# Eight projection strips that start from raw tokens instead of normalized ones

## The chip, the cores and the metric

The kernel runs as one program on one core of one Trainium2 chip. The metric is the time of one execution in microseconds (us), as the device measures it. Three executions of the kernel before gave a median of 1279.75 us (1279.38 to 1280.37). The engines are TensorE (PE in the profile, its weight loads PEld), VectorE (DVE), ScalarE (ACT), GpSimd (POOL) and SyncE (SP), which issues most of the DMA transfers.

## The reference, cut to what matters

Two transformer blocks run on 512 tokens of width 1024. Only the beginning of the first one bears on this change:

```python
def rmsnorm(x, gain):
    y = x * lax.rsqrt(jnp.mean(x * x, axis=-1, keepdims=True) + NORM_EPS)
    return y * gain

h = rmsnorm(x, mix_norm[l])          # x: 512 tokens x 1024
proj = h @ w_in[l]                   # 1024 x 3840
q, k, v, su, sv, g_a, g_b = jnp.split(proj, splits, axis=-1)
# chunked_spatial_gating(su, sv, ...):
u = jax.nn.gelu(su)
v = rmsnorm(jax.nn.gelu(sv), sgu_gain)
```

Everything is fp32 and is computed to more than one rounded pass of the matmul: each operand is split into a rounded part ("high") and a rest ("low"), and three products are added, high x high, low x high and high x low.

## The kernel before, in words

Activations lie transposed: 128 features on the partitions, 512 tokens along a row, 8 such tiles `k` for the width of 1024. A weight strip `n` is 1024 x 128 numbers. Its way is: SP loads it into `w_raw` (two slots, two transfers of 256 KB), DVE rounds it into `w_high` (`make_high`, L365), POOL subtracts to get `w_low` (`make_low`, L370), and PE runs 8 x 3 matmuls of 512 columns (`product`, L391 to L393). `w_high` and `w_low` have four slots. SP may load strip `n` once `w_low` of strip `n - 2` is made. The semaphores `high_made`, `low_made` and `strip_used` count these steps. Every engine works through a list that is written out in the program, and waits at semaphores; nothing reorders it.

The start runs so. Tokens come in four pieces `x_tok` of 128. DVE and ACT sum their squares, ACT makes the four columns of roots `x_root`, DVE and ACT multiply the tokens by them, and PE turns the result (`row_turn`, L864). ACT multiplies by the gain `mix_gain` while it rounds to `h_high` (L1658), DVE makes `h_low` (L2197). Besides, PE turns the raw tokens too (`raw_turn`, L853), since the residual `x_t` is wanted later. Then PE runs strips 0 to 7 (the `su` and `sv` columns), with some small transposes between them: the rows of constants and the 16 meta tokens before strip 1 (L898 to L903), the sum of the meta tokens' squares before strip 2 (L910), the mixing weights after strip 5 (L922). ACT applies GELU straight from PSUM to `uv` (L1671). For strips 4 to 7 (`sv`) a second norm follows: ACT squares (L1679), POOL adds two of them at a time (L664, with `make_low` of strip 10 between the two additions), and PE sums over partitions (`sv_sums`, L939 and L941) after the first three `k` of strip 9. Strips 8 to 13 are `k`, `v` and `q`. Four banks of PSUM, `ps[:, n % 4, :]`, are used in turn by strips 0 to 7, so that strip 4 has to wait until bank 0 has been read.

## Time and profile before

| what | value |
|---|---|
| median of three executions | 1279.75 us |
| the profiled execution | 1279.36 us |
| its span, first to last instruction | 1277.6 us |
| PE busy | 1257.2 us (98%) |
| DVE, ACT, POOL busy | 710.7, 467.3, 627.4 us |
| mean granted TensorE clock | 0.999 |

The profiled execution lies 0.39 us under the median, and 1.76 us of it lie outside the span. PE is busy from its first real work to the end, so the time is what PE has to do, plus the stretches in which it stands still. The beginning, about 30 us, and the stretch from 65 to 73 us are where it stands still near this change.

### The profile page before, as it was taken

The page shows a single profiled execution, that of the slowest core. Times are in us where ns is not written, and L with a number is a line of the kernel's source. Part 1 is how long each engine was busy: PE and PEld are TensorE (multiplying, and loading weights), DVE is VectorE, ACT ScalarE, POOL GpSimd, SP SyncE. Part 2 cuts the span into 40 slices and gives each one's busy share as a digit, 9 for nine tenths or more (in the row PEclk, how much of TensorE's full clock was granted, in tenths as well). Part 3 has the DMA queues.
Part 4 walks back from the last instruction along what each step waited for, and adds up shares of the span by engine and source line. Part 5 has one row for each costly group of instructions (what it writes and reads, how often), then busy time and mean ns, then how long its engine had stood idle before and what let it go on. Part 6 is the DMA issues. An engine that isn't in the chain of part 4 may idle for free.

```text
span 1277.6 us, 19955 instructions
## 1 busy us (share of the span) xinstructions
PE 1257.2 (98%) x6772; PEld 1032.4 (81%) x6772; DVE 710.7 (56%) x1380; ACT 467.3 (37%) x1010; POOL 627.4 (49%) x418
## 2 busy tenths in 40 slices
PE   7999999999999999999999999999999999999998
PEld 6877777877788888888888888888888888888876
DVE  5236654566855455443224788778643665665641
ACT  4233433412422222221113566566402555555531
POOL 5442333338354434445663153444347877777722
PEclk9999999999999999999999999999999999999999
DMA  7322222223232333233333221111133322222213
GB/s 205 100 66 70 81 81 78 57 88 109 83 115 82 99 99 97 84 90 97 102 91 100 67 56 44 49 33 50 50 98 95 96 79 79 78 78 78 66 34 99
DMA packets 190611, 105.42 MB, mean 83 GB/s; under 512 B 19174, under 2 KB 186444, under 8 KB 190556
## 3 DMA queue, kind: packets, MB, share of 16 engines
q1 hardware_dynamic: 189748, 102.82, 28.4%
q0 software_dynamic: 432, 0.69, 0.2%
q10 hardware_dynamic: 376, 1.18, 0.2%
q8 instruction: 33, 0.54, 0.2%
q14 instruction: 22, 0.18, 0.1%
HBM read 102.57 MB, written 2.10 MB: 82 GB/s over the span
## 4 chain that ended last, share of the span: by engine, by line
PE 90%; DVE 5%; ACT 2%; issue 1%; POOL 1%; DMA 1%; ACTq 0%; DVEq 0%
PE ps L391 20%; PE ps L392 20%; PE ps L393 20%; PE ps L422 9%; PE ps L1453 1%; PE ps L1535 1%; PE ps L1537 1%; PE ps L1536 1%; PE ps L1484 1%; PE ps L1464 1%; PE ps L1208 1%; PE ps L404 1%; PE ps L405 1%; PE ps L408 1%; DMA x_tok<-in_x_dram 1%
## 5 line engine op out<-in xcount | busy, mean ns | idle before, releaser
L370 POOL TENSOR_TENSOR w_low<-w_raw,w_high 128x1024 fp32r<-128x1024 f32 x180 | 440.1, 2448 | 445.5 <-DVE w_high L365 440.3
L391 PE MATMUL ps<-h_high,w_high 128*128 128x512 f32 x810 | 326.4, 403 | 0.5 <-DVE h_low L524 0.4
L392 PE MATMUL ps<-h_low,w_high 128*128 128x512 f32 x810 | 319.9, 395 | 0.0
L393 PE MATMUL ps<-h_high,w_low 128*128 128x512 f32 x810 | 318.8, 394 | 0.0
L365 DVE CAST w_high<-w_raw 128x1024 fp32r<-128x1024 f32 x183 | 152.4, 834 | 111.8 <-DMA w_raw<-in_w_down_dram 34.1
L391 PEld LDWEIGHTS ps<-h_high,w_high 128*128 128x128 f32 x810 | 152.2, 188 | 37.7 <-issue 3.0
L393 PEld LDWEIGHTS ps<-h_high,w_low 128*128 128x128 f32 x810 | 152.3, 188 | 34.8
L392 PEld LDWEIGHTS ps<-h_low,w_high 128*128 128x128 f32 x810 | 152.1, 188 | 33.1 <-issue 1.7
L1788 ACT ACTIVATE z<-ps,cv 128x512 f32<-128x512 f32 x42 | 32.7, 778 | 148.3 <-PE ps L393 148.3
L2407 DVE SCALAR_TENSOR_TENSOR z<-ps,cv,z 128x511 f32<-128x511 f32 x42 | 31.5, 749 | 92.8 <-ACT z L1788 92.8
L392 PE MATMUL ps<-m_low,w_high 128*128 128x512 f32 x176 | 69.4, 395 | 0.0
L393 PE MATMUL ps<-m_high,w_low 128*128 128x512 f32 x176 | 69.4, 395 | 0.0
L391 PE MATMUL ps<-m_high,w_high 128*128 128x512 f32 x176 | 69.4, 394 | 0.0
L422 PE MATMUL ps<-h_high,w_high 128*128 128x264 f32 x304 | 64.8, 294 | 0.3 <-ACT nv_end L2096 0.3
L422 PE MATMUL ps<-h_high,w_low 128*128 128x264 f32 x304 | 61.7, 284 | 0.0
L422 PE MATMUL ps<-h_low,w_high 128*128 128x264 f32 x304 | 61.5, 284 | 0.0
L770 POOL TENSOR_TENSOR nb<-rel,mask 128x128 f32<-128x128 f32 (+1 forms) x96 | 53.4, 599 | 0.2 <-DMA rel<-in_rel_bias_dram 0.2
L422 PEld LDWEIGHTS ps<-h_high,w_high 128*128 128x128 f32 x304 | 48.4, 189 | 5.2 <-issue 2.5
L2041 ACT ACTIVATE np_<-ps 128x256 f32<-128x256 f32 (+1 forms) x32 | 15.7, 491 | 93.2 <-PE ps L1468 93.2
L422 PEld LDWEIGHTS ps<-h_low,w_high 128*128 128x128 f32 x304 | 47.0, 188 | 0.0
L422 PEld LDWEIGHTS ps<-h_high,w_low 128*128 128x128 f32 x304 | 46.9, 188 | 0.0
L2714 DVE TENSOR_SCALAR ne<-ne,nm 128x272 f32<-128x272 f32 (+2 forms) x64 | 46.2, 762 | 1.1
(393 smaller groups left out, 2392.4 us busy)
## 6 DMA issues: line engine op xcount, KB each, us to landing
...
```

The source lines that it names most:

```text
L365: dve.tensor_copy(w_high[:, n % RING, :], w_raw[:, n % RAW, :]).then_inc(high_made, 1)
L370: pool.tensor_tensor(w_low[:, n % RING, :], w_raw[:, n % RAW, :], w_high[:, n % RING, :].bitcast(F32), ALU.subtract).then_inc(low_made, 1)
L391: pe.matmul(acc, wh, mh, start=first and k == 0, stop=False)
L392: pe.matmul(acc, wh, ml, start=False, stop=False)
L393: done = pe.matmul(acc, wl, mh, start=False, stop=last and k == tiles - 1)
L404: pe.matmul(ps[:, banks[o], :], w_high[:, slot, at], mh, start=k == 0, stop=False)
L422: done = pe.matmul(ps[:, bank + h, 0:HALF], wt, mt[:, k, h * HALF:h * HALF + HALF], start=one_, stop=end)
L770: pool.tensor_tensor(to, half_tiles(rel[:, h, :], r, n), half_tiles(mask[:], m, n), ALU.add)\
L1788: act.activation(z[:, m, :], src, ACT.Identity, scale=cv[:, bass.ds(i * 2 + (C_CONV + 2 * 2 * FT + ct), 1)], bias=cv[:, bass.ds(i * 2 + (C ...
L2041: act.activation(np_[:, a:a + n, :, t % 2 * P:(t % 2 + 1) * P], turned(n), ACT.Copy)\
L2407: dve.scalar_tensor_tensor(z[:, m, 1:S], src[:, 0:S - 1], cv[:, bass.ds(i * 2 + (C_CONV + 2 * FT + ct), 1)], z[:, m, 1:S], ALU.mult, ALU.a ...
L2714: p = dve.tensor_scalar(ne[:, t % 2, h, 0:w], ne[:, t % 2, h, 0:w], nm[:, t % 2, 2, h:h + 1], None, ALU.mult)
```

## The change

The tokens' roots are a factor of each column of the result, since `(x * root) @ w` is `(x @ w) * root`. The changed kernel therefore multiplies the raw tokens, times the gain, and puts the roots to the finished columns. In detail:

- PE turns the raw tokens once, in two halves of 256 tokens (`turn_half`). The turned tokens lie in banks 4 to 7. ACT rounds them times the gain into `a_high` (buffers that are otherwise unused until later), DVE makes `a_low`, ACT copies `x_t`.
- Strips 0 and 1 run as matmuls of 256 columns (`raw_pass`): both strips on the first half, then the second half is turned, then both strips on the second half. Strips 2 to 7 run at 512 columns on `a_high` and `a_low`.
- Token pieces 2 and 3 are loaded behind strips 0 and 1 on SP's queue, strip 2 ahead of the small rows of constants.
- In the middle of strip 2 stand the transposes of constants and meta tokens, and four fp32 matmuls that spread the four columns `x_root` over 128 partitions as rows. DVE copies these to `v_f`.
- For each of the strips 0 to 7 DVE multiplies the PSUM bank by `v_f` into `uv` (semaphore `sv_normed`), and ACT applies GELU to `uv` in place. PE's waits for a free bank are now on `sv_normed`.
- Behind the multiplications of strips 0 to 3, two at a time, DVE and ACT make the eight tiles of the normalized tokens `h_high` and `h_low` (`norm_dve`, `norm_highs`), which strips 8 and following use.
- `make_high` of strips 5 to 11 stands ahead of the multiplications of strips 1 to 7 on DVE; strip 11's was behind the loop before.

The diff, with removed code left out where it is only replaced (it is shown above):

```diff
--- before.py
+++ after.py
+HALF_S = S // 2
+RAW_PARTS = 2 * KT
...
-            for k in range(KT):
-                act.wait_ge(s["norm_scaled"], 8 * t - 4 + k + 1)
+            norm_highs(act, t, n, high)
+        def norm_highs(act, t, n, high, ks=(0, KT)):
+            for k in range(*ks):
+                act.wait_ge(s["norm_scaled"], 8 * t + k + 1)
                 act.activation(high(k), scaled[:, k % 2, 0:n], ACT.Copy).then_inc(s["norm_high"], 1)
...
+        def norm_dve(dve, t, src, gain, by, n, high, low, ks=(0, KT)):
+            for k in range(ks[0], ks[1] + 1):
+                if k < ks[1]:
+                    if 8 * t + k >= 2:
                         dve.wait_ge(s["norm_low"], 8 * t + k - 1)
-                    dve.scalar_tensor_tensor(scaled[:, k % 2, 0:n], src(k), col(gain + k), root[:, 0, 0:n],
+                    dve.scalar_tensor_tensor(scaled[:, k % 2, 0:n], src(k), gain(k), by[:, 0:n],
                                              ALU.mult, ALU.mult).then_inc(s["norm_scaled"], 1)
-                if k >= 1:
+                if k > ks[0]:
                     dve.wait_ge(s["norm_high"], 8 * t + k)
                     dve.tensor_tensor(low(k - 1), scaled[:, (k - 1) % 2, 0:n], high(k - 1).bitcast(F32),
...
+        def of_half(h, k):
+            return ps[:, 4 + k // 2, k % 2 * HALF_S:(k % 2 + 1) * HALF_S]
+        def raw_at(parts, h, k):
+            return parts[:, k, h * HALF_S:(h + 1) * HALF_S]
...
-            sp.dma_start(x_tok[:, 2, :], x[0, 2 * P:3 * P, :]).then_inc(s["x_rest_in"], 16)
             sp.wait_ge(s["x_in"], 32)
             for n in range(RAW):
                 load_strip(sp, n)
+            for t in (2, 3):
+                sp.dma_start(x_tok[:, t, :], x[0, t * P:(t + 1) * P, :]).then_inc(s["x_rest_in"], 16)
+            load_strip(sp, RAW)
...
-            for n in range(RAW, 4):
-                load_strip(sp, n)
-            sp.wait_ge(s["in_turned"], KT + 3)
+            load_strip(sp, RAW + 1)
+            sp.wait_ge(s["norm_sq"], 4)
             sp.dma_start(ws_raw[:], w_s[0].rearrange("g i j -> i g j")).then_inc(s["meta_in"], 16)
...
+            def turn_half(h):
+                pe.wait_ge(s[("x_in", "x_rest_in")[h]], 32)
+                if h == 0:
+                    pe.wait_ge(s["cols_ready"], 1)
+                for b in range(4):
+                    if h:
+                        pe.wait_ge(s["x_ready"], b + 1)
+                    for k in (2 * b, 2 * b + 1):
+                        for t in range(2):
+                            mm = pe.transpose(ps[:, 4 + b, (k % 2 * 2 + t) * P:(k % 2 * 2 + t + 1) * P],
+                                              x_tok[:, 2 * h + t, k * P:(k + 1) * P], ident[:])
                     mm.then_inc(s["in_turned"], 1)
-            pe.wait_ge(s["norm_scaled"], 2)
+            def raw_pass(h, n, k, w, part, first=False, last=False):
+                return pe.matmul(ps[:, n, h * HALF_S:(h + 1) * HALF_S], w[:, n, k * P:(k + 1) * P], raw_at(part, h, k),
+                                 start=first, stop=last)
+            turn_half(0)
+            pe.wait_ge(high_made, 1)
+            for k in range(KT):
+                pe.wait_ge(s["raw_high"], k + 1)
+                raw_pass(0, 0, k, w_high, a_high, first=k == 0)
             for k in range(4):
...
+                pe.wait_ge(s["raw_low"], k + 1)
+                raw_pass(0, 0, k, w_high, a_low)
+            pe.wait_ge(low_made, 1)
             for k in range(KT):
-                t = pe.transpose(ps[:, 6, k * META:(k + 1) * META], meta_tok[:, k * P:(k + 1) * P],
-                                 ident[0:META, 0:META])
-            t.then_inc(s["in_turned"], 1)
+                raw_pass(0, 0, k, w_low, a_high)
+            pe.wait_ge(high_made, 2)
+            for k in range(KT):
+                raw_pass(0, 1, k, w_high, a_high, first=k == 0)
+            for k in range(4, KT):
+                pe.wait_ge(s["raw_low"], k + 1)
+                raw_pass(0, 0, k, w_high, a_low, last=k == KT - 1)
+            for k in range(KT):
+                raw_pass(0, 1, k, w_high, a_low)
             pe.wait_ge(low_made, 2)
...
+            for k in range(KT):
+                raw_pass(0, 1, k, w_low, a_high, last=k == KT - 1)
+            turn_half(1)
+            for k in range(KT):
+                pe.wait_ge(s["raw_high"], KT + k + 1)
+                for n in range(2):
+                    raw_pass(1, n, k, w_high, a_high, first=k == 0)
+                    raw_pass(1, n, k, w_low, a_high)
+                pe.wait_ge(s["raw_low"], KT + k + 1)
+                for n in range(2):
+                    mm = raw_pass(1, n, k, w_high, a_low, last=k == KT - 1)
+                    if k == KT - 1:
+                        mm.then_inc(strip_used, 1)
+            def raw(k):
+                return a_high[:, k, :], a_low[:, k, :]
+            for n in range(2, N_QKV):
                 pe.wait_ge(low_made, n + 1)
+                if n >= 4:
+                    pe.wait_ge(s["sv_normed"], n - 3)
+                cut = 4 if n == 2 else KT
+                mm = product(pe, ps[:, n % 4, :], n, 0, P, KT, raw, ks=(0, cut))
                 if n == 2:
-                    pe.wait_ge(s["meta_ready"], 1)
-                if n >= 4:
-                    pe.wait_ge(s["gelu_done"], n - 3)
-                product(pe, ps[:, n % 4, :], n, 0, P, KT, hx).then_inc(strip_used, 1)
+                    pe.wait_ge(s["x_ready"], 8)
+                    pe.wait_ge(s["consts_in"], 16 * N_CONST)
+                    pe.wait_ge(s["more_in"], 16 * N_EARLY)
...
+                    pe.wait_ge(s["norm_root"], 4)
+                    for t in range(4):
+                        mm = pe.matmul(ps[:, 5, t * P:(t + 1) * P], x_root[:, t:t + 1].broadcast_to([P, P]), ident[:],
+                                       start=True, stop=True)
+                    mm.then_inc(s["in_turned"], 1)
+                    mm = product(pe, ps[:, n % 4, :], n, 0, P, KT, raw, ks=(cut, KT))
+                mm.then_inc(strip_used, 1)
+                if n == 2:
+                    pe.wait_ge(s["norm_sq"], 12)
+                    pe.matmul(ps[:, 4, 0:META], ones[:], sq[:, 1, 0:META], start=True, stop=True)\
+                        .then_inc(s["norm_sum"], 8)
                 if n == 5:
...
+            pe.wait_ge(s["norm_low"], 16)
             pe.wait_ge(s["more_in"], 16 * N_MORE)
...
                 if m == 1:
-                    pe.wait_ge(s["gelu_done"], 8)
+                    pe.wait_ge(s["sv_normed"], 8)
...
-            act.dma_start(x_tok[:, 3, :], x[0, 3 * P:S, :]).then_inc(s["x_rest_in"], 16)
             act.preload_act_table_set("natural_log_exp_and_others")
             act.wait_ge(s["ones_set"], 2)
...
+            def raw_highs(h):
+                for k in range(KT):
+                    act.wait_ge(s["in_turned"], 1 + 4 * h + k // 2 + 1)
+                    act.activation(raw_at(a_high, h, k), of_half(h, k), ACT.Copy, scale=mix_gain[:, k:k + 1])\
+                        .then_inc(s["raw_high"], 1)
+            def keep_x(h):
+                for b in range(4):
+                    act.wait_ge(s["raw_low"], KT * h + 2 * b + 2)
+                    act.activation(x_t[:, 2 * b:2 * b + 2, h * HALF_S:(h + 1) * HALF_S],
+                                   ps[:, 4 + b, :].rearrange("p (k q) -> p k q", q=HALF_S), ACT.Copy)\
+                        .then_inc(s["x_ready"], 1)
+            def square_token(t):
                 act.activation(xh_tok[:, t, :], x_tok[:, t, :], ACT.Square, accum_out=x_sum[:, t:t + 1])\
                     .then_inc(s["norm_sq"], 1)
...
+            act.wait_ge(s["cols_ready"], 1)
+            raw_highs(0)
+            keep_x(0)
+            act.wait_ge(s["x_in"], 32)
+            square_token(0)
+            raw_highs(1)
+            act.wait_ge(s["x_rest_in"], 32)
+            square_token(2)
+            keep_x(1)
+            act.wait_ge(s["norm_sq"], 4)
+            act.activation(x_root[:], x_sum[:], ACT.Ln, bias=eps[:, 0:1], scale=1.0 / D).then_inc(s["norm_root"], 2)
+            act.wait_ge(s["norm_root"], 2)
+            act.activation(x_root[:], x_root[:], ACT.Exp, scale=-0.5).then_inc(s["norm_root"], 2)
+            act.wait_ge(s["in_turned"], 11)
...
+            norm_highs(act, 0, META, lambda k: h_high[:, k, 0:META])
             for n in range(8):
-                act.wait_ge(strip_used, N_SGU + n + 1)
-                act.activation(uv[:, n, :], ps[:, n % 4, :], ACT.Gelu_apprx_tanh).then_inc(s["gelu_done"], 1)
+                act.wait_ge(s["sv_normed"], n + 1)
+                act.activation(uv[:, n, :], uv[:, n, :], ACT.Gelu_apprx_tanh).then_inc(s["gelu_done"], 1)
+                if n < 4:
+                    norm_highs(act, 1, S, hh, (2 * n, 2 * n + 2))
...
+            def raw_lows(h, ks):
+                for k in ks:
+                    dve.wait_ge(s["raw_high"], KT * h + 2 * (k // 2) + 2)
+                    dve.scalar_tensor_tensor(raw_at(a_low, h, k), of_half(h, k), mix_gain[:, k:k + 1],
+                                             raw_at(a_high, h, k).bitcast(F32), ALU.mult, ALU.subtract)\
+                        .then_inc(s["raw_low"], 1)
             def square_token(t, ready):
                 dve.wait_ge(ready, 32)
                 dve.tensor_tensor_reduce(xh_tok[:, t, :], x_tok[:, t, :], x_tok[:, t, :], 1.0, 0.0, ALU.mult, ALU.add,
                                          x_sum[:, t:t + 1]).then_inc(s["norm_sq"], 1)
+            make_high(dve, 0)
+            raw_lows(0, range(4))
+            make_high(dve, 1)
+            raw_lows(0, range(4, KT))
             square_token(1, s["x_in"])
-            scaled_tokens(0, (0, 1))
+            make_high(dve, 2)
+            raw_lows(1, range(KT))
             square_token(3, s["x_rest_in"])
...
+            make_high(dve, 3)
+            dve.wait_ge(s["in_turned"], 10)
             dve.tensor_copy(cv[:], ps[:, 7, 0:C_V + V_ROWS]).then_inc(s["cols_ready"], 1)
             dve.wait_ge(s["cols_ready"], 2)
             dve.tensor_scalar(aq_gain[:], col(V_AQ), HD ** -0.5, None, ALU.mult).then_inc(s["gain_ready"], 1)
             dve.tensor_scalar(nq_gain[:], col(V_NQ), HD ** -0.5, None, ALU.mult).then_inc(s["gain_ready"], 1)
-            make_high(dve, 3)
             for k, v in enumerate((V_QPE, V_QN)):
                 dve.tensor_scalar(mq_gain[:, k:k + 1], col(v), MLA_SCALE, None, ALU.mult).then_inc(s["gain_ready"], 1)
+            dve.wait_ge(s["in_turned"], 12)
+            dve.tensor_copy(v_f[:], ps[:, 5, :]).then_inc(s["cols_ready"], 1)
             dve.wait_ge(s["norm_sq"], 8)
             dve.tensor_reduce(sq[:, 1, 0:META], sq[:, 0, 0:KT * META].rearrange("p (k m) -> p m k", m=META), AX.X,
                               ALU.add).then_inc(s["norm_sq"], 4)
-            norm_dve(dve, 1, lambda k: meta_t[:, k, :], V_N2, META,
+            make_high(dve, 4)
+            dve.wait_ge(s["norm_root"], 6)
+            norm_dve(dve, 0, lambda k: meta_t[:, k, :], lambda k: col(V_N2 + k), root[:, 0, :], META,
                      lambda k: h_high[:, k, 0:META], lambda k: h_low[:, k, 0:META])
-
-            for n in range(N_SGU + 1, N_QKV):
-                make_high(dve, n + 3)
+            dve.wait_ge(s["cols_ready"], 3)
+            for n in range(8):
+                if n:
+                    make_high(dve, n + 4)
+                dve.wait_ge(strip_used, n + 1)
+                dve.tensor_tensor(uv[:, n, :], ps[:, n % 4, :], v_f[:], ALU.mult).then_inc(s["sv_normed"], 1)
+                if n < 4:
+                    norm_dve(dve, 1, xs, lambda k: mix_gain[:, k:k + 1], v_f, S, hh, hl, (2 * n, 2 * n + 2))
...
-            make_high(dve, N_QKV + 3)
```

DVE's list from strip 3 on, in the kernel before. Casts to `w_high` are `make_high`; `scaled<-meta_t` and `h_low` with 16 columns belong to the meta tokens.

```order
L524 TENSOR_TENSOR h_low<-scaled,h_high 128x16 [waits norm_high] x2
L365 CAST w_high<-w_raw 128x1024 [waits strip_used,strip_landed_0]
L365 CAST w_high<-w_raw 128x1024 [waits strip_used,strip_landed_1]
L365 CAST w_high<-w_raw 128x1024 [waits strip_used,strip_landed_0]
L365 CAST w_high<-w_raw 128x1024 [waits strip_used,strip_landed_1]
L365 CAST w_high<-w_raw 128x1024 [waits strip_used,strip_landed_0]
L365 CAST w_high<-w_raw 128x1024 [waits strip_used,strip_landed_1]
L365 CAST w_high<-w_raw 128x1024 [waits strip_used,strip_landed_0]
L365 CAST w_high<-w_raw 128x1024 [waits strip_landed_1,strip_used,more_in,gain_ready]
L2247 SCALAR_TENSOR_TENSOR uv<-uv,cv,root 128x512 [waits sv_root]
```

The same place in the changed kernel, cut to strips 0, 1 and 5 to 7 (L367 is `make_high`, L2256 the multiplication by the roots):

```order
L2256 TENSOR_TENSOR uv<-ps,v_f 128x512 [waits strip_used,cols_ready]
L524 SCALAR_TENSOR_TENSOR scaled<-x_t,mix_gain,v_f 128x512 [waits norm_low] x2
L528 TENSOR_TENSOR h_low<-scaled,h_high 128x512 [waits norm_high] x2
L367 CAST w_high<-w_raw 128x1024 [waits strip_used,strip_landed_1]
L2256 TENSOR_TENSOR uv<-ps,v_f 128x512 [waits strip_used]
L524 SCALAR_TENSOR_TENSOR scaled<-x_t,mix_gain,v_f 128x512 [waits norm_low] x2
...
L367 CAST w_high<-w_raw 128x1024 [waits strip_used,strip_landed_1]
L2256 TENSOR_TENSOR uv<-ps,v_f 128x512 [waits strip_used]
L367 CAST w_high<-w_raw 128x1024 [waits strip_used,strip_landed_0]
L2256 TENSOR_TENSOR uv<-ps,v_f 128x512 [waits strip_used]
L367 CAST w_high<-w_raw 128x1024 [waits strip_used,strip_landed_1]
L2256 TENSOR_TENSOR uv<-ps,v_f 128x512 [waits strip_used]
```

Before, nothing but casts stood between the meta tokens and the second norm. Now each multiplication stands behind a cast, and those of strips 0 to 3 are followed by four tile operations each.

PE's list at the start of the changed kernel (L872 turns raw tokens, L878 is a pass of 256 columns):

```order
L872 MATMUL ps<-ident,x_tok 128x128 [waits cols_ready,x_in]
L872 MATMUL ps<-ident,x_tok 128x128 x15
L878 MATMUL ps<-a_high,w_high 128x256 [waits raw_high,high_made]
L878 MATMUL ps<-a_high,w_high 128x256 [waits raw_high] x7
L878 MATMUL ps<-a_low,w_high 128x256 [waits raw_low] x4
L878 MATMUL ps<-a_high,w_low 128x256 [waits low_made]
L878 MATMUL ps<-a_high,w_low 128x256 x7
L878 MATMUL ps<-a_high,w_high 128x256 [waits high_made]
L878 MATMUL ps<-a_high,w_high 128x256 x7
```

Before, it began with 16 transposes of raw tokens (L853) and 32 of scaled ones (L864) ahead of the first product; the 32 and the two waits for `norm_scaled` are gone, and the first product now waits for strip 0's `high_made`.

## Rows read from the trace of the kernel before

**Rows 1.** The page, part 1: busy time and share of the span.

```profile
PE 1257.2 (98%) x6772; PEld 1032.4 (81%) x6772; DVE 710.7 (56%) x1380; ACT 467.3 (37%) x1010; POOL 627.4 (49%) x418
```

**Rows 2.** Waits of PE, 0 to 135 us: total, times, longest.

```profile
PE ps L849 <- DMA ident<-in_c_ident_dram: 4.9, 1, 4.9
PE ps L864 <- ACT xh_tok L1655: 1.8, 1, 1.8
...
PE ps L939 <- POOL root L664: 0.5, 1, 0.5
```

**Rows 3.** Timeline, 0 to 35 us: start, duration, engine, line, work, count.

```profile
6.20 2.15 SPq L354 DMA_DIRECT2D w_raw<-in_w_in_dram  x4
6.22 3.28 PE L853 MATMUL ps<-ident,x_tok 128*128 128x128 f32 x16 [1.04 <-DMA x_tok<-in_x_dram]
...
16.61 4.17 SPq L354 DMA_DIRECT2D w_raw<-in_w_in_dram  x4
...
20.29 1.91 PE L853 MATMUL ps<-ident,x_tok 128*128 128x128 f32 x16
20.49 0.69 DVE L365 CAST w_high<-w_raw 128x1024 fp32r<-128x1024 f32 x1 [0.49 <-DMA w_raw<-in_w_in_dram]
...
23.20 0.14 PEld L898 LDWEIGHTS ps<-ident,rows_a 88*128 88x128 f32 x1
...
24.45 0.19 PEld L391 LDWEIGHTS ps<-h_high,w_high 128*128 128x128 f32 x1
...
29.91 0.42 PEld L910 LDWEIGHTS ps<-sq,ones 128*128 128x128 f32 x2
...
30.28 0.48 PE L391 MATMUL ps<-h_high,w_high 128*128 128x512 f32 x1
...
34.17 1.29 DVE L365 CAST w_high<-w_raw 128x1024 fp32r<-128x1024 f32 x2
```

**Rows 4.** Busy time of each engine from 30.28 to 64.82 us.

```profile
30.28:64.82 34.54, 34.54 (x156) 28.14 (x155) 8.05 (x23) 7.41 (x18) 15.20 (x7) 1.00 0.41 106
```

**Rows 5.** The chain, other stretches: start, duration, what.

```profile
81.88 0.86 PE ps L933 x2
...
701.41 0.75 DVE scaled L2451
702.16 0.61 DVE h_low L2455
...
719.03 3.66 PE ps L422 x30
```

**Rows 6.** Timeline: POOL and DVE side by side at three places.

```profile
237.60 0.69 DVE L2362 TENSOR_TENSOR scaled<-gates 128x512 f32<-128x512 f32 x1
...
241.38 2.41 POOL L370 TENSOR_TENSOR w_low<-w_raw,w_high 128x1024 fp32r<-128x1024 f32 x1 [13.91 <-DVE w_high L365]
...
242.53 1.81 DVE L2362 TENSOR_TENSOR scaled<-gates 128x512 f32<-128x512 f32 x1
...
282.94 2.40 POOL L370 TENSOR_TENSOR w_low<-w_raw,w_high 128x1024 fp32r<-128x1024 f32 x1 [6.64 <-DVE w_high L365]
283.05 2.84 DVE L2380 SCALAR_TENSOR_TENSOR m_low<-x_t,cv,m_high 128x512 fp32r<-128x512 f32 x1 [0.19 <-ACT m_high L1773]
```

**Rows 7.** The chain that ended last, 64 to 73 us.

```profile
64.82 0.60 ACT uv L1671
65.44 1.28 ACT L1674
66.73 1.16 ACT sq L1679 x2
...
67.96 1.30 POOL root L664
69.31 2.28 issue
71.59 1.30 POOL root L664
72.94 1.13 PE ps L939 x2
```

**Rows 8.** Timeline of POOL in that stretch.

```profile
69.23 2.40 POOL L370 TENSOR_TENSOR w_low<-w_raw,w_high 128x1024 fp32r<-128x1024 f32 x1
```

137 lines of the change are left out of this document (25 added, 112 removed).

## The prediction, written before the changed kernel ran

> **What bounds the kernel now.** I read the page first, then the waits of PE over the first 135 us, the timeline of the beginning, and the chain from 60 to 76 us. The page shows PE busy for 98% of the span [rows 1], so a change pays only where PE stands still or where it has less to do. PE's waits near the change are few: 4.9 us for the first data, 1.8 us for the scaled tokens, and 0.5 us at the sum over partitions of the second norm [rows 2]. From 30.28 us (start of strip 2) to 64.82 us (end of strip 7) PE is busy in all 34.54 us [rows 4]. In that stretch there are six strips and eight transposes. A warm transpose costs 1.91 / 16 = 0.119 us [rows 3], so a strip takes (34.54 - 0.95) / 6 = 5.60 us. Behind strip 7 the reader sees a chain that PE nearly waits for: GELU, a table load, two squares, an addition on POOL, then `make_low` of strip 10, the other addition, and at 72.94 us the sum on PE [rows 7, 8]. From the start of the last GELU to that sum it is 8.12 us; PE arrives 0.5 us too early [rows 2]. This chain has no slack: whatever comes late at the last GELU is paid in full.
>
> **The front: what is saved.** The price of the beginning is the moment at which PE starts strip 3, since from there both kernels have the same 512-column work. Before, it is 30.28 + 5.60 = 35.88 us. After:
>
> - SP issues strips 0 and 1 when tokens 0 and 1 have landed. Before, that is 6.20 us [rows 3]. Pieces 2 and 3 no longer travel beside them, so it can't be later for that reason; I take 5.7 us, bounds 5.2 and 6.2.
> - Strip 2's issue at 16.61 us was followed by a cast that had waited for it and began at 20.49 us [rows 3]: 3.9 us from issue to use on a quiet queue. So strip 0's cast starts at 9.6 and ends at 10.3 us; `make_low` takes 2.4 us [rows 8] and ends at 12.7 us. Before, strips 0 and 1 queued behind token pieces; if they take two us longer here too, all that follows is two us later.
> - Until 12.7 us PE has turned the first half, and has run the 12 passes that need no `w_low`. The 32 transposes of scaled tokens and their wait of 1.8 us are gone from its list. Behind 12.7 us there are 36 passes, 16 transposes (1.91 us), and 48 passes. A pass of 264 columns took 3.66 / 30 = 0.122 us [rows 5]; for 256 I take 0.1185. That makes 84 x 0.1185 + 1.91 = 11.9 us, and strip 2 starts at 24.6 us. ACT and DVE have 0.7 us of PE's time for each of the eight tiles of the second half and need less than one half-width operation each, so I cost them at nothing; if they fell behind, it would be by their own pace, not more than 1 us.
> - Strip 2 is 5.60 us; the constants' transposes, 1.25 us (23.20 to 24.45 [rows 3]), stand inside it now and before strip 1 then; the sum of the meta squares is 0.35 us in both (29.91 to 30.28 [rows 3]). New are the four fp32 matmuls of the roots: one of 512 columns is 0.86 us [rows 5], four of 128 together the same, 0.86 us.
>
> Strip 3 starts at 24.6 + 5.60 + 1.25 + 0.35 + 0.86 = 32.7 us. The front saves 35.9 - 32.7 = 3.2 us; bounds 1.2 (strip 0 two us late) and 3.8.
>
> **The middle: what is lost.** Call strip 3's start E. Strip 7 ends at T = E + 5 x 5.60 + 0.95 = E + 28.95. DVE had only casts here. Now it has per strip a cast, a multiplication, and for strips 0 to 3 two `scaled` and two `h_low` operations. Their quiet prices are 0.65 (two casts in 1.29 [rows 3]), about 0.62, 0.75 and 0.61 us [rows 5]. One round would be 4.1 us, less than a strip.
>
> They aren't quiet. Each round's cast releases POOL's `make_low`, and `scaled<-x_t,mix_gain,v_f` with two inputs in SBUF follows at once. The trace has that pair: `scaled<-gates` takes 0.69 us when POOL is idle, and 1.81 us when `make_low` runs; it ends at 244.34, and `make_low` at 243.79 us. `m_low<-x_t,cv,m_high`, an operation of the very kind, took 2.84 us and ended 0.55 us behind the `make_low` that began 0.11 us before it [rows 6]. So DVE waits for POOL's 2.4 us and then does its work. A round is then 0.65 cast + 0.08 + 2.4 + 0.55 + 0.75 + two `h_low`, 1.25 with their semaphores: 5.7 to 5.8 us.
>
> The Trainium skill's page "SBUF — State Buffer", section "Who interferes with whom", says that a VectorE instruction with two SBUF inputs contends with a GpSimd instruction that reads SBUF, and that the later one is blocked entirely. The trace agrees with both halves.
>
> Counted from E (all of it moves with PE):
>
> - DVE leaves the meta tokens at 3.9 (30.28 to 34.17 [rows 3]), multiplies strip 0 until 4.5, and finishes the first pair at 7.6, because ACT has to load GELU's table (1.28 us [rows 7]) and run a GELU before it can round.
> - Casts of strips 5, 6, 7, 8 end at 8.2, 14.0, 19.8, 25.7; `make_low` follows each by 2.5 us. PE needs strips 5 to 8 at 11.2, 17.8, 23.4, 28.95, and has them 0.5 to 1.5 us before. No stall yet.
> - Strip 9: its cast waits for `make_low` of strip 8 (28.2), ends 28.8; its `make_low` ends 31.3. Only then may SP load strip 11: 3.9 us, 35.2. Its cast ends at 35.8, and the multiplication of strip 7 stands behind it on DVE: 36.5 = T + 7.5.
>
> Before, the last GELU began at T. It now begins 7.5 us later, and 8.12 us behind that comes PE's sum. PE stands about 2 us at strip 9, which waits for `sv_normed`, and about 6 us at the sum, where it stood 0.5 us. The loss is 7.5 us. Bounds: 1.35 us, if strip 11 is in place when strip 7 ends (cast plus multiplication), and 8.5 us with a load of 4.9 us.
>
> **The clock.** PE's first 16 transposes, after it had done nothing, took 3.28 us, the same 16 later 1.91 us [rows 3]: it starts at the lower of its two levels, 1.2 GHz, and the difference is 1.37 us. The gap of 1.8 us at 11 us [rows 2] was not followed by slow work. A gap of 6 us lies between; I take one more fall, 1.37 us, bounds 0 and 2.8 (twice).
>
> The Trainium skill's page "TensorE: Matmul & The Clock Gate", section "What's actually happening", has the array at half rate when it has been idle and back at full rate after sustained work; by it the long gap costs a fall. No run here shows it yet.
>
> **Sum.** Against the profiled execution: 1279.36 - 3.2 + 7.5 + 1.4 = 1285.0 us. The median of the runs is 0.39 us higher, so 1285.4 us.
>
> **Rivals.**
>
> 1. *DVE isn't held by POOL* (or the rounds are hidden otherwise). Rounds of 4.1 us: casts of strips 8 and 9 end at 20.2 and 23.2, `make_low` of 9 at 25.7, strip 11 lands at 29.6, its cast ends at 30.2, the multiplication at 30.9 = T + 1.9. The long gap is then about 2.5 us and the clock holds. 1279.75 - 3.2 + 2.0 = 1278.6 us. For it: the same operations in the later norms run at 0.75 and 0.61 us [rows 5], but there POOL has nothing to do. Against it: rows 6. This one is not slower than before. Chance 0.15.
> 2. *The last load comes in time and the front does better*: tokens at 5.2 us, strip 11's cast ready at T. 1279.75 - 3.7 + 1.35 = 1277.4 us. Chance 0.08.
> 3. *The clock doesn't fall*: 1284.0 us. Chance 0.22.
> 4. *The front is lost*: strip 0 arrives like before behind other transfers, or PE's clock falls between its short passes from 9 to 13 us; saving 1.2 us: 1287.4 us. Chance 0.12.
>
> My forecast has 0.43. A measurement here can tell 0.2%, 2.6 us, from no change. Rival 1 lies within it, rival 2 at its edge: faster 0.06, same 0.18, slower 0.76. The range, 1279.0 to 1288.0, takes in the forecast, rivals 3 and 4 and the mixtures between rival 1 and the forecast, in which only some rounds are held; the likeliest case alone has 1284 to 1287.
>
> **What would show it.** In the profile after: strip 2 starts near 24.6 and strip 3 near 32.7 us; no waits of PE between 13 and 60 us over 0.5 us. `scaled<-x_t,mix_gain,v_f` of the second, third and fourth pair takes over 2 us for the first of two, at 0.75 for the other. The last multiplication ends about 7.5 us behind strip 7, with DVE's last cast waiting for a DMA; PE waits about 2 us for DVE and 6 us for POOL, and matmuls behind the gap start 0.43 us apart instead of 0.23. Wrong would be: a last GELU within 3 us of strip 7's end (rival 1 or 2), a strip 2 later than 26 us (rival 4), or a stall before strip 5, whose margin of 0.5 us is the thinnest.

## The result, and the profile after

| | median | lowest to highest | ratio to before |
|---|---|---|---|
| before | 1279.57 us (4 runs) | 1279.29 to 1280.37 | |
| after | 1287.91 us (4 runs) | 1287.25 to 1288.98 | 1.0065 (95%: 1.0053 to 1.0077) |

The change makes the kernel 8.3 us slower. The profiled execution took 1288.1 us, 1286.3 us of it the span, with a mean clock of 0.996. The page's first part, to be read beside [rows 1], shows that PE's busy time is nearly the same and the span 8.7 us longer, so on balance the loss is standing time (about 2 us of slow work, shown below, hide in a busy time that has lost 32 transposes):

```profile
PE 1257.5 (98%) x6796; PEld 1034.3 (80%) x6796; DVE 732.1 (57%) x1407; ACT 475.6 (37%) x1030; POOL 626.2 (49%) x418
```

The waits of PE from 0 to 140 us (waiting tile and line, releaser, total, times, longest), to be read beside [rows 2]:

```profile
PE ps L969 <- POOL root L676: 5.6, 1, 5.6
PE ps L861 <- DMA ident<-in_c_ident_dram: 4.8, 1, 4.8
PE ps L393 <- DVE uv L2256: 2.2, 1, 2.2
PE ps L872 <- DMA x_tok<-in_x_dram: 1.7, 1, 1.7
PE ps L878 <- DVE w_high L367: 1.0, 1, 1.0
...
PE ps L878 <- POOL w_low L372: 0.5, 1, 0.5
```

The wait of 0.5 us at the sum over partitions has become 5.6 us, and a wait of 2.2 us at strip 9 is new. The front has lost its wait for the scaled tokens and now has three that concern tokens and strip 0.

**The front.** Timeline of the changed kernel (start, duration, engine, line, work, count, idle time before and its releaser), to be read beside [rows 3]:

```profile
6.73 2.05 SPq L356 DMA_DIRECT2D w_raw<-in_w_in_dram  x4
...
10.72 0.69 DVE L367 CAST w_high<-w_raw 128x1024 fp32r<-128x1024 f32 x1 [5.43 <-DMA w_raw<-in_w_in_dram]
11.50 2.38 POOL L372 TENSOR_TENSOR w_low<-w_raw,w_high 128x1024 fp32r<-128x1024 f32 x1 [6.21 <-DVE w_high L367]
...
25.81 0.39 PE L393 MATMUL ps<-a_high,w_high 128*128 128x512 f32 x1
...
33.54 0.48 PE L393 MATMUL ps<-a_high,w_high 128*128 128x512 f32 x1
```

The tokens landed at 6.7 us, when SP went on to strips 0 and 1; from there strip 0 needs 4.0 us to its cast and 3.2 us more to the end of `w_low`. The last two rows are the starts of strips 2 and 3. Before, strip 3 started here:

```profile
35.94 0.40 PE L391 MATMUL ps<-h_high,w_high 128*128 128x512 f32 x1
```

The front is thus 2.40 us ahead (the prediction had worked out 35.88 us for this start).

**The middle.** DVE's timeline, one round and the end; before, nothing but the casts stood here [rows 3]:

```profile
41.41 0.69 DVE L367 CAST w_high<-w_raw 128x1024 fp32r<-128x1024 f32 x1
...
42.61 3.19 DVE L524 SCALAR_TENSOR_TENSOR scaled<-x_t,mix_gain,v_f 128x512 f32<-128x512 f32 x2
...
47.11 0.69 DVE L367 CAST w_high<-w_raw 128x1024 fp32r<-128x1024 f32 x1
...
59.82 2.39 DVE L367 CAST w_high<-w_raw 128x1024 fp32r<-128x1024 f32 x1
...
66.03 0.69 DVE L367 CAST w_high<-w_raw 128x1024 fp32r<-128x1024 f32 x1 [3.22 <-DMA w_raw<-in_w_in_dram]
68.92 0.69 DVE L367 CAST w_high<-w_raw 128x1024 fp32r<-128x1024 f32 x1 [1.60 <-DMA w_raw<-in_w_in_dram]
69.53 0.68 DVE L2256 TENSOR_TENSOR uv<-ps,v_f 128x512 f32<-128x512 f32 x1
```

POOL in the same stretch (the same columns):

```profile
42.17 2.41 POOL L372 TENSOR_TENSOR w_low<-w_raw,w_high 128x1024 fp32r<-128x1024 f32 x1 [7.30 <-DVE w_high L367]
...
59.25 2.41 POOL L372 TENSOR_TENSOR w_low<-w_raw,w_high 128x1024 fp32r<-128x1024 f32 x1 [3.29 <-DVE w_high L367]
```

The two scalings together take 3.19 us instead of twice 0.75 [rows 5]: POOL has begun `w_low` 0.44 us before them, and the first scaling ends behind it. One round (cast to cast) is 5.70 us.

The chain to the sum, from which [rows 7] is the piece before (start, duration, what):

```profile
62.29 2.41 POOL w_low L372
...
65.12 3.77 DMA w_raw<-in_w_in_dram
...
68.92 0.69 DVE w_high L367
...
70.24 0.63 ACT uv L1710
...
76.94 1.28 POOL root L676
...
78.26 2.08 PE ps L969 x2
80.33 1.71 PE ps L971 x2
```

The last multiplication stands behind the cast of strip 11, which waits for its load, which waits for `w_low` of strip 9. And PE's sums take 2.08 and 1.71 us where they took 1.13 [rows 7] and, for the two behind, 0.86. The granted clock of that stretch stands third from the right in the rows of the windows (before it the stretch's length and the busy times of PE, PEld, DVE, ACT and POOL, behind it the DMA share and GB/s):

```profile
75.00:78.00 3.00, 0.00 (x0) 0.00 (x0) 0.00 (x0) 1.83 (x3) 3.00 (x2) 0.58 0.00 0
78.00:82.00 4.00, 3.74 (x5) 1.68 (x6) 0.00 (x0) 0.00 (x0) 2.50 (x2) 0.50 0.68 145
```

It is at the lower of its two levels, 1.2 GHz, for all of the sums.

**Where the 8.7 us are.** Since the work behind the sums is the same in every kernel here, I compare the starts of two `w_low` operations on POOL that belong to the same strips in all of them, near 86 and 583 us. Before:

```profile
85.58 2.77 POOL L370 TENSOR_TENSOR w_low<-w_raw,w_high 128x1024 fp32r<-128x1024 f32 x1 [10.39 <-DVE w_high L365]
...
583.15 2.41 POOL L370 TENSOR_TENSOR w_low<-w_raw,w_high 128x1024 fp32r<-128x1024 f32 x1 [4.23 <-DVE w_high L365]
```

After:

```profile
92.89 2.77 POOL L372 TENSOR_TENSOR w_low<-w_raw,w_high 128x1024 fp32r<-128x1024 f32 x1 [12.39 <-DVE w_high L367]
...
590.89 2.41 POOL L372 TENSOR_TENSOR w_low<-w_raw,w_high 128x1024 fp32r<-128x1024 f32 x1 [4.54 <-DVE w_high L367]
```

The kernel is 7.31 us late at the first, 7.74 at the second, and 8.74 at the end (1288.1 - 1279.36). So 7.3 us belong to the changed stretch. They are -2.4 (front), +7.7 (PE's sum starts 5.32 us later, 78.26 against 72.94, from a front 2.40 us earlier), and +2.0 (clock, measured below as 1.96): 7.3. Below, "shift" is the place against these two rows of before.

### The profile page after: what moved, and what is told of

Its sections match the earlier page's. It is cut to its first block, busy times and chain, and to the rows that moved or that the text cites. A ratio compares the mean times of both kernels' runs of the same rounds, so it can differ in the third digit from the quotient of the medians.

```text
span 1286.3 us, 20052 instructions
## 1 busy us (share of the span) xinstructions
PE 1257.5 (98%) x6796; PEld 1034.3 (80%) x6796; DVE 732.1 (57%) x1407; ACT 475.6 (37%) x1030; POOL 626.2 (49%) x418
## 4 chain that ended last, share of the span: by engine, by line
PE 86%; DVE 6%; ACT 2%; POOL 2%; DMA 2%; issue 2%; SPq 0%; ACTq 0%; DVEq 0%
PE ps L393 18%; PE ps L394 18%; PE ps L395 18%; PE ps L424 9%; PE ps L1483 1%; PE ps L1565 1%; PE ps L1567 1%; PE ps L1566 1%; POOL w_low L372 1%; DVE scaled L524 1%; PE ps L1514 1%; PE ps L1494 1%; DMA w_raw<-in_w_in_dram 1%; PE ps L1238 1%; PE ps L878 1%
## 5 line engine op out<-in xcount | busy, mean ns | idle before, releaser
L372 POOL TENSOR_TENSOR w_low<-w_raw,w_high 128x1024 fp32r<-128x1024 f32 x180 | 439.4, 2443 | 459.2 <-DVE w_high L367 453.9
L393 PE MATMUL ps<-h_high,w_high 128*128 128x512 f32 x752 | 304.1, 404 | 2.7 <-DVE uv L2256 2.2
L394 PE MATMUL ps<-h_low,w_high 128*128 128x512 f32 x752 | 297.2, 395 | 0.0
L395 PE MATMUL ps<-h_high,w_low 128*128 128x512 f32 x752 | 296.1, 394 | 0.0
L367 DVE CAST w_high<-w_raw 128x1024 fp32r<-128x1024 f32 x183 | 156.7, 857 | 100.0 <-DMA w_raw<-in_w_in_dram 36.5
L393 PEld LDWEIGHTS ps<-h_high,w_high 128*128 128x128 f32 x752 | 141.6, 188 | 38.0 <-issue 6.0
L395 PEld LDWEIGHTS ps<-h_high,w_low 128*128 128x128 f32 x752 | 141.5, 188 | 32.2
L394 PEld LDWEIGHTS ps<-h_low,w_high 128*128 128x128 f32 x752 | 141.5, 188 | 30.9 <-issue 1.9
L424 PE MATMUL ps<-h_high,w_high 128*128 128x264 f32 x304 | 64.8, 294 | 1.1 <-POOL w_low L372 0.8
L424 PE MATMUL ps<-h_high,w_low 128*128 128x264 f32 x304 | 61.7, 285 | 0.0
L424 PE MATMUL ps<-h_low,w_high 128*128 128x264 f32 x304 | 61.6, 284 | 0.0
L424 PEld LDWEIGHTS ps<-h_high,w_high 128*128 128x128 f32 x304 | 48.3, 189 | 6.2 <-issue 3.5
L424 PEld LDWEIGHTS ps<-h_low,w_high 128*128 128x128 f32 x304 | 47.0, 188 | 0.0
L424 PEld LDWEIGHTS ps<-h_high,w_low 128*128 128x128 f32 x304 | 47.0, 188 | 0.0
L1848 ACT ACTIVATE x_t<-z 128x512 f32<-128x512 f32 x8 | 9.8, 1222 | 100.5 <-DVE z L2474 100.5
```

Of the source, the lines that this page charges most:

```text
L367: dve.tensor_copy(w_high[:, n % RING, :], w_raw[:, n % RAW, :]).then_inc(high_made, 1)
L372: pool.tensor_tensor(w_low[:, n % RING, :], w_raw[:, n % RAW, :], w_high[:, n % RING, :].bitcast(F32), ALU.subtract).then_inc(low_made, 1)
L393: pe.matmul(acc, wh, mh, start=first and k == 0, stop=False)
L394: pe.matmul(acc, wh, ml, start=False, stop=False)
L395: done = pe.matmul(acc, wl, mh, start=False, stop=last and k == tiles - 1)
L424: done = pe.matmul(ps[:, bank + h, 0:HALF], wt, mt[:, k, h * HALF:h * HALF + HALF], start=one_, stop=end)
```

## The experiments

Each ran beside the kernel before on its chip. The measured numbers stand in one table; the last two columns are shifts. Strip 3, the wait and the sums are each kernel's rows like those shown above.

| kernel | ratio (95%) | strip 3 starts | wait before sums | sums | at 86 us | at 583 us |
|---|---|---|---|---|---|---|
| changed | 1.0065 (1.0053 to 1.0077) | 33.54 | 5.6 | 2.08 + 1.71 | +7.31 | +7.74 |
| cast 11 behind | 1.0039 (1.0025 to 1.0053) | 33.04 | 5.6 | 2.07 + 1.64 | +4.05 | +3.98 |
| roots from PSUM | 1.0025 (1.0016 to 1.0035) | 33.01 | 3.7 | 1.15 + 1.71 | +2.09 | +2.01 |
| both | 0.9992 (0.9983 to 1.0002) | 33.46 | 1.3 | 1.12 + 0.86 | -1.46 | -1.53 |
| gap filled | 1.0049 (1.0032 to 1.0066) | 33.50 | 1.5, behind the added matmuls | 1.13 + 0.86 | +5.35 | +5.52 |
| strip 0 early | 1.0049 (1.0033 to 1.0064) | 31.77 | 5.6 | 2.08 + 1.71 | +5.71 | +5.62 |
| tokens ahead | 1.0086 (1.0071 to 1.0102) | 35.16 | 5.5 | 2.08 + 1.71 | +9.38 | +9.28 |
| three edits | 0.9984 (0.9975 to 0.9993) | 33.12 | none | 1.05 + 0.86 | -3.22 | -3.26 |
| four edits | 0.9964 (0.9951 to 0.9978) | 33.94 | none | 0.99 + 0.86 | -2.46 | -2.53 |
| changed, again | 1.0064 (1.0050 to 1.0078) | 34.17 | 5.6 | 2.08 + 1.71 | +8.25 | +8.56 |
| four edits, again | 0.9974 (0.9965 to 0.9983) | 31.43 | none | 0.97 + 0.86 | -4.98 | -5.05 |

### The cast of strip 11 behind the loop

```diff
-                if n:
+                if 1 <= n < 7:
                     make_high(dve, n + 4)
...
+            make_high(dve, N_QKV + 3)
```

> The cast of strip 11 goes back behind the loop of the multiplications, as in the kernel before; everything else stays as in the changed kernel. Theory (the last multiplication stands behind a cast whose strip lands late): in the changed kernel the cast of strip 11 began at 68.92 us and the last multiplication ended 36.0 us behind the start of strip 3. Without that cast it stands behind strip 10's, which began at 66.03 us, so it ends about 33.5 us behind the start of strip 3, 2.5 us earlier. PE's wait of 2.2 us before strip 9 goes, the wait before the sums of the second norm stays near 6 us (both ends move together), the clock still falls behind it. Time 1287.9 - 2.5 = 1285.4 us. Rival (the order of casts on DVE does not matter, the chain is late from the GELUs on ACT or from POOL): the sums come where they came, 1287.9 us.

Measured: 1286.24 us beside 1280.82 of the kernel before, which was 1.25 us slower on this chip than beside the changed kernel; ratios and places are the fairer measure in this and the next three. The place moved by 3.26 us at 86 us, 0.50 of which came in the front, so 2.76 us for the edit, where 2.5 were expected. DVE's rows show the last two multiplications together behind strip 10's cast, which waits for its load:

```profile
65.33 0.69 DVE L367 CAST w_high<-w_raw 128x1024 fp32r<-128x1024 f32 x1 [3.02 <-DMA w_raw<-in_w_in_dram]
65.94 1.28 DVE L2256 TENSOR_TENSOR uv<-ps,v_f 128x512 f32<-128x512 f32 x2
```

PE's wait at strip 9 is gone, that before the sums is still 5.6 us, since both ends of it moved. The median is 0.8 us above the expected 1285.4; by the ratio it would be 1284.6. The order of casts matters; the rival falls.

### The roots read from PSUM

```diff
-                    norm_dve(dve, 1, xs, lambda k: mix_gain[:, k:k + 1], v_f, S, hh, hl, (2 * n, 2 * n + 2))
+                    norm_dve(dve, 1, xs, lambda k: mix_gain[:, k:k + 1], ps[:, 5, :], S, hh, hl, (2 * n, 2 * n + 2))
```

> The tokens' normalization behind strips 0 to 3 reads the spread roots from their PSUM bank instead of the copy in SBUF, so that its scaling has one operand in SBUF and not two. Same work, same order. Theory (an operation of DVE with two operands in SBUF stands still while POOL makes w_low): the pair of scalings takes about 1.5 instead of 3.2 us in strips 1 to 3, the rounds of DVE shrink from 5.7 to about 4.4 us, the last multiplication ends about 32 us behind strip 3's start instead of 36.0, PE's wait before the sums shrinks from 5.6 to about 4 us and the wait before strip 9 goes. Time 1287.9 - 4.3 = 1283.6 us if the clock still falls behind the shorter gap, 1281.7 us if it holds. Rival (the 3.2 us are not POOL's doing but a wait for ACT's rounding or for a buffer): the pair keeps 3.2 us and the time stays at 1287.9 us. Second rival (reading PSUM beside PE's writes is slower): the pair takes over 2 us each time, 1286 us or more.

Measured: 1284.14 us beside 1280.82; the place moved by 5.22 us, 0.53 of which in the front. DVE's rows in this kernel:

```profile
42.07 1.40 DVE L524 SCALAR_TENSOR_TENSOR scaled<-x_t,mix_gain,ps 128x512 f32<-128x512 f32 x2
45.13 0.68 DVE L367 CAST w_high<-w_raw 128x1024 fp32r<-128x1024 f32 x1
...
49.37 0.68 DVE L367 CAST w_high<-w_raw 128x1024 fp32r<-128x1024 f32 x1
```

POOL's beside them:

```profile
41.64 2.42 POOL L372 TENSOR_TENSOR w_low<-w_raw,w_high 128x1024 fp32r<-128x1024 f32 x1 [7.30 <-DVE w_high L367]
```

POOL's `w_low` runs from 41.64 to 44.06 us, across both scalings, and they take 1.40 us together. The only difference to 3.19 us is where one operand lies. The round shrinks to 4.24 us. Both rivals fall: it was neither a buffer nor ACT, and reading PSUM costs nothing extra.

Neither time expected for the clock (1283.6 if it fell, 1281.7 if it held) was met: by the ratio the time would be 1282.8 us. The wait was 3.7 us, and the clock fell only when PE worked again. The windows of this kernel:

```profile
74.00:75.00 1.00, 1.00 (x3) 0.42 (x2) 0.00 (x0) 0.00 (x0) 1.00 (x1) 0.68 1.25 282
75.00:78.00 3.00, 3.00 (x8) 1.88 (x7) 0.25 (x1) 1.70 (x3) 0.63 (x1) 0.54 0.60 125
78.00:79.00 1.00, 1.00 (x6) 0.82 (x5) 1.00 (x2) 0.11 (x1) 0.00 (x0) 1.00 0.81 184
```

The first sum (two rows of the profile), from 73.38 us, still ran at full speed (1.15 us), the second did not (1.71 us). From the start of the sums to the place at 86 us this kernel needs 14.29 us (73.38 to 87.67), where the changed kernel needs 14.63 (78.26 to 92.89) and the kernel before 12.64 (72.94 to 85.58): the late fall still cost about 1.6 us.

### Both edits

> Both edits together: the cast of strip 11 behind the loop, and the roots read from their PSUM bank. Theory: the last multiplication comes 6.8 us earlier than in the changed kernel, PE's wait before the sums is about 1.6 us, and the two sums take 1.13 and 0.86 us again, not 2.08 and 1.71. Time 1287.9 - 6.8 - 1.9 = 1279.2 us, level with the kernel before. If the slow matmuls behind the gap have nothing to do with its length, they stay at 2.08 and 1.71 us: 1281.1 us. Rival (one of the two causes hides the other, and only one of them is worth anything): 1283 to 1285 us.

Measured: 1279.97 us beside 1280.82. The place moved by 8.77 us (expected 6.8 + 1.9 = 8.7). Chain of this kernel:

```profile
70.14 1.26 POOL root L676
...
71.45 1.12 PE ps L969 x2
72.58 0.86 PE ps L971 x2
```

Behind a wait of 1.3 us the sums run at full speed. The two edits are worth more together (8.7 without the front) than one by one (2.8 + 4.7), because only together do they leave a gap short enough for the clock: from the sums to the place at 86 us it is 12.67 us here (71.45 to 84.12), 14.29 with the roots alone and 14.36 with the cast alone (75.27 to 89.63).

### The gap filled

```diff
+                        for _ in range(10):
+                            pe.matmul(ps[:, 3, :], w_high[:, n % RING, 0:P], hx(0)[0], start=True, stop=True)
+                        pe.wait_ge(s["sv_sum"], 1)
+                        for _ in range(8):
+                            pe.matmul(ps[:, 3, :], w_high[:, n % RING, 0:P], hx(0)[0], start=True, stop=True)
```

> PE runs 18 matmuls of 512 columns that nobody uses, in the gap before the sums of the second norm: ten at once, eight when the first sum of squares is there. The chain that PE waits for is the same. Theory of the clock (the sums and the first matmuls behind the gap run at the lower level because PE stood still for 5.6 us): the two sums take 1.13 and 0.86 us, the granted clock from 70 to 85 us is near 1, and the time is 1287.9 - 1.9 = 1286.0 us. Rival (the slow matmuls are slow for another reason, for instance because their operands come from ACT and POOL at that moment): sums stay at 2.08 and 1.71 us, the time at 1287.9 us, or up to 1 us more where the added matmuls outlast the wait.

Measured: 1287.63 us beside 1280.82. The sums begin at 78.28 us, as in the changed kernel (78.26), and the chain reads:

```profile
76.97 1.28 POOL root L676
78.28 1.13 PE ps L969 x2
79.41 0.86 PE ps L971 x2
```

Windows of the same kernel:

```profile
74.00:78.00 4.00, 2.82 (x13) 1.83 (x11) 0.00 (x0) 2.07 (x3) 4.00 (x3) 1.00 0.00 0
```

The place at 86 us moved by 1.96 us, the expected 1.9, with the chain untouched; the clock term is thus measured alone. The ratio falls by as much, 1.0049 against 1.0065 or 2.0 us, but the two intervals overlap, so it is the trace that settles this. The median is 1.6 us above the expected time. The slower chip (1.25 us) can account for most of it, and a late part that isn't edited adds to it: between 583 us and the end its profiled execution (1287.8 us) lost 2.9 us more (8.44 - 5.52).

### Strip 0 early

```diff
-            sp.wait_ge(s["x_in"], 32)
             for n in range(RAW):
                 load_strip(sp, n)
```

> SP no longer waits for tokens 0 and 1 before it issues strips 0 and 1 (nor, behind them, tokens 2 and 3); all else is as in the changed kernel. There strips 0 and 1 were issued at 6.73 us and strip 0's cast began at 10.72 us, so the front hangs on the landing of the tokens twice. Theory (the front is bound by strip 0's way: issue, 4.0 us, cast, 2.4 us of w_low): strip 0's cast begins 2 to 3 us earlier, strip 3 starts 1.0 to 2.5 us earlier, and all behind it moves with PE, so the time is 1285.4 to 1286.9 us against the changed kernel's 1287.9. Rival (the transfers share the same engines, so the tokens land as much later as the strip lands earlier, or PE's first passes run at the lower clock): strip 3 starts where it did or up to 1 us later, 1287.9 to 1289 us.

Measured: 1285.92 us beside 1279.73. The timeline shows strips 0 and 1 issued at once, and the cast 1.74 us earlier; the tokens landed at 6.1 us, no later. I had expected the cast 2 to 3 us earlier:

```profile
1.74 2.55 SPq L356 DMA_DIRECT2D w_raw<-in_w_in_dram  x4
...
8.98 0.69 DVE L367 CAST w_high<-w_raw 128x1024 fp32r<-128x1024 f32 x1 [3.27 <-DMA w_raw<-in_w_in_dram]
```

Strip 3 starts 1.77 us earlier: what the cast gains, PE gains. The front hangs on strip 0's way, as the prediction's sum had it.

### Tokens 2 and 3 ahead of strips 0 and 1

The two lines that load tokens 2 and 3 are put ahead of the wait for tokens 0 and 1, so they are issued at 1.74 us; the text below says behind that wait, which isn't how the kernel was written.

> Tokens 2 and 3 are issued by SP ahead of strips 0 and 1, behind the wait for tokens 0 and 1. Theory (strip 0's landing sets the front, and a strip behind 1 MB of tokens lands later): strip 0's cast begins at 12.5 us or later instead of 10.72 us, strip 3 starts 1.0 to 2.0 us later, the time is 1288.9 to 1289.9 us. Rival (PE's own work sets the front, the strip has slack): strip 3 starts at 33.5 us as in the changed kernel, 1287.9 us.

Measured: 1290.8 us beside 1279.73. The cast of strip 0:

```profile
11.62 0.69 DVE L367 CAST w_high<-w_raw 128x1024 fp32r<-128x1024 f32 x1 [6.24 <-DMA w_raw<-in_w_in_dram]
```

Strips 0 and 1 were issued at 6.18 us here and needed 5.4 us to that cast instead of 4.0. That is less than the 12.5 us that I expected, and the time more than the 1 to 2 us (2.9 us, or 2.7 by the ratio). Strip 3 starts 1.62 us later and the place at 86 us is 2.07 us later: strip 0 has no slack, the rival falls. Of the 1.62 us the later cast is 0.90. The rest, 0.7 us, goes with a fall of the clock: PE had stood 2.5 us before its first pass at 12.37 us, the granted clock is 0.58, 0.50, 0.50 and 0.72 in the four stretches of 1 us from 13 to 17 us, and the eight passes behind `w_low` took 1.98 us instead of 1.23. The profiled execution was the quickest of its four and only 1.25 us slower than that of the changed kernel (1289.35 against 1288.1), so no trace shows where the rest of the medians' 2.9 us lies. A strip 0 that arrives later behind other transfers is the first half of the prediction's rival 4, brought about by this edit.

### Three edits, and four

The third edit moves `make_low` of strip 10 on POOL from between the two additions to before both; the fourth is the one of "strip 0 early".

```diff
-                make_low(pool, n)
+                if n != 10:
+                    make_low(pool, n)
+                if n == 9:
+                    make_low(pool, 10)
```

> The cast of strip 11 behind the loop, the roots read from their PSUM bank, and on POOL w_low of strip 10 ahead of the two additions of the second norm instead of between them. With the first two alone the wait before the sums was 1.3 us, and between POOL's two additions lay w_low of strip 10 (2.4 us), for whose end the second addition waited. Theory (POOL's order is the last thing on this chain): with w_low of strip 10 done before the last square is there, the second addition starts as soon as its squares do, the wait of 1.3 us goes, no fall of the clock. Time 1.3 us below the kernel with the two edits alone, 1278.7 us against 1280.8 of the kernel before on that chip (0.998). Rival (the squares on ACT set the second addition, or w_low of strip 10 delays the first addition by as much): no change against the kernel with two edits, 1280.0 us (0.999).

> All of these: cast of strip 11 behind the loop, roots from PSUM, w_low of strip 10 ahead of the additions, and strips 0 and 1 issued without a wait for the tokens. Theory: the gains lie at different places of one path and add up, because everything behind strip 3 hangs on PE and moves with it: 1.0 to 2.5 us below the kernel with three edits, 1276.2 to 1277.7 us where the kernel before has 1280.8 (ratio 0.9965 to 0.998). Rival (an earlier front is lost again because a DVE round or a strip's load then ends last): level with the kernel with three edits.

Measured: 1278.04 us with three and 1275.67 us with four, beside 1279.73. POOL's rows with three edits:

```profile
66.25 1.31 POOL L679 TENSOR_TENSOR root<-sq 128x512 f32<-128x512 f32 x1 [1.92 <-ACT sq L1723]
68.36 1.30 POOL L679 TENSOR_TENSOR root<-sq,root 128x512 f32<-128x512 f32 x1 [0.80 <-ACT sq L1723]
```

The second addition now waits for ACT's squares and not for `w_low`, and PE doesn't wait for either. The place moved by 1.76 us against two edits, of which 0.34 in the front. The fourth edit brought 2.4 us more in the medians, though not in its profiled execution (1278.19 us, the slowest of five). There strip 0 was cast at 10.45 us, 0.10 us later than with three edits, and PE's first passes ran slowly:

```profile
11.20 2.08 PE L880 MATMUL ps<-a_high,w_high 128*128 128x256 f32 x8 [1.11 <-DVE w_high L367]
```

The same eight passes took 1.21 us with three edits, and strip 3 started 0.82 us later than there. So this kernel and the changed one were run again.

### The changed kernel and the one with four edits, again

> The changed kernel itself, beside the one with four edits on one chip. Shifts read from the traces put it 8.7 us behind the kernel before at the end, of which 7.7 us are there at 583 us; the first of these is the change, the rest may be this one execution's. Theory: the place is 7.3 to 7.7 us behind again at 86 us and 583 us; what comes later lies between 0 and 2 us and differs from execution to execution. Ratio to the kernel before 1.0065. Rival (the later microsecond belongs to the change): again 1.0 us or more between 583 us and the end.

> The kernel with four edits once more, since its profiled execution (1278.19 us) was the slowest of its five (median 1275.67 us) and its strip 0 was cast at 10.45 us, no earlier than without the fourth edit, while the same edit alone had it at 8.98 us. Theory (the transfers of tokens and strips 0 and 1 share the DMA engines, and which lands first differs by execution): a ratio of 0.9955 to 0.9975 to the kernel before, and a cast of strip 0 anywhere from 9 to 10.5 us; strip 3 starts as much earlier as the cast. Rival (the first series was lucky): ratio 0.998 or more, as with three edits.

Measured: 1288.16 us and 1276.18 us beside 1279.57. The front of the second:

```profile
8.66 0.69 DVE L367 CAST w_high<-w_raw 128x1024 fp32r<-128x1024 f32 x1 [3.28 <-DMA w_raw<-in_w_in_dram]
```

Strip 0 is cast at 8.66 us here and strip 3 starts at 31.43; the same program had 10.45 and 33.94 us before. The cast lies 1.79 us earlier, a little ahead of the 9 to 10.5 us expected. Strip 3 lies 2.51 us earlier, and not by as much as the cast, which was expected: the first passes were quicker too (the first eight 1.81 us against 2.08, the eight behind `w_low` 1.21 against 1.60). What the theory says of the order isn't shown: in both executions tokens 0 and 1 landed first, at 6.2 and 6.4 us. The version with four edits is faster than both kernels, by 0.26 to 0.36% than the one before.

The changed kernel stood at +8.25 at 86 us, not at 7.3 to 7.7 as I expected. Of the 0.94 us that it is later than in its first profile, 0.63 are there at strip 3: the cast of strip 0 came 0.10 us later, and the first passes ran slowly.

```profile
10.82 0.69 DVE L367 CAST w_high<-w_raw 128x1024 fp32r<-128x1024 f32 x1 [5.55 <-DMA w_raw<-in_w_in_dram]
11.56 2.07 PE L878 MATMUL ps<-a_high,w_high 128*128 128x256 f32 x8 [0.86 <-DVE w_high L367]
```

Eight passes take 2.07 us; in the first profile it was 1.21 us. Behind 583 us 1.2 us were added (1289.17 - 1279.36 - 8.56). That does not refute the rival of this run, and I take it up in the next section.

## Why the prediction was right, step by step

Forecast 1285.4 us with a range to 1288.0; measured 1287.9. The direction and the mechanism held. That the median lies inside the range is luck: it is 0.09 us under the upper end, two of the four executions (1288.1 and 1288.98) lie above it, and so does the median of the second series (1288.16). Against the profiled execution the forecast was 1285.0 us and 1288.1 came; the 3.1 us between them are four terms that all missed to the same side: 0.8 us in the front, 0.2 in the middle, 0.6 in the clock and 1.4 behind the change.

- **The front, 3.2 us forecast, 2.4 found** (1.8 in the second profile, 2.4 to 2.9 in the other kernels with the same front). The step that failed is the first: tokens 0 and 1 landed at 6.7 us, not at 5.7, and outside the bounds of 5.2 and 6.2. The upper bound was the single trace of before, on the argument that with less beside them they can't be later; over the executions they landed between 5.9 and 7.0 us. That less beside them brings them earlier isn't shown either: with tokens 2 and 3 ahead of the wait they landed at 6.2 us. Everything behind it came as worked out: 4.0 us from issue to cast (3.9 forecast), strip 2's first matmul 11.9 us behind the end of `w_low` at 13.9 us, and 7.7 us more to strip 3 (8.1 forecast). Strip 0 early and tokens ahead show that this way is what the front hangs on.
- **The middle, 7.5 us forecast, 7.7 found.** The round of 5.7 to 5.8 us is 5.70. The stretches "about 2 us at strip 9" and "about 6 us at the sum" are 2.2 and 5.6. Roots from PSUM shows that POOL's `w_low` holds the scalings; cast 11 behind shows that the last cast, which waits for its load, holds the last multiplication.

  The Trainium skill's page "SBUF — State Buffer", section "Who interferes with whom", says that a VectorE instruction with at most one SBUF input and outside the two-port modes doesn't contend. Roots from PSUM agrees: 1.40 us for the pair beside a running `w_low`.
- **The clock, 1.4 us forecast, 2.0 found.** One fall, as forecast; the size was taken from 16 transposes of 128 columns, but what ran slowly were the two fp32 matmuls of 512 columns (four rows in the profile) and the first passes behind them. 2.08 + 1.71 against 1.13 + 0.86 us is 1.8 us by itself. Gap filled takes the term away and gains 1.96 us. Rival 3 (no fall) is false.
- **Behind the change, nothing forecast, 1.4 us found.** 0.4 us lie between 86 and 583 us, where PE's wait at `w_low` (L406) grew from 0.3 to 0.8 us, and 1.0 us behind. In the ten experiments the last part was between 0.1 us (cast 11 behind) and 2.9 us (gap filled), 1.2 us in the mean, against the one trace of before. So it isn't a fixed price of the change. In the changed kernel 0.8 us of it is one wait (`PE ps L424 <- POOL w_low L372: 0.8`), at 973 us: that `w_low` stands on POOL behind twelve additions that had themselves waited 1.0 us for the table `rel` to land, against 0.2 us in the kernel before. Cast 11 behind doesn't have PE's wait. The kernels with both edits, with four and with four again have it (0.8, 1.2 and 0.5 us), though at 583 us they are ahead of the kernel before, so a later place isn't what brings it. That the single trace of before is a quick one in this part fits this, but isn't shown; the runs of the kernel before alone had medians of 1279.57 to 1280.82 us on different chips.

The rivals: 1 (DVE not held) and 2 (last load in time) would have needed a last GELU within 3 us of strip 7's end; it began at 70.24 us, 7.9 us behind (strip 8 had begun at 62.38). Rival 4's second form, a clock fall among the first passes, did occur. In tokens ahead the granted clock shows it. In the second profile of the changed kernel, in gap filled and in four edits only the durations tell of it, beside a granted clock of 1.00. It cost 0.5 us in the first (strip 3 0.63 us later, the cast 0.10), 0.8 us in gap filled (cast at 9.92, 0.80 us earlier, strip 3 at 33.50, 0.04 us earlier) and 0.7 us in four edits (strip 3 0.82 us later than with three, the cast 0.10), and it isn't in the changed kernel's first profile, which the forecast is held against. What decides it stays open: PE had stood 0.86 us before the slow passes of the second profile, and as long before the quick ones of cast 11 behind.
